# Up projections that alternate between two PSUM banks, warm-up matmuls at the start, and a new order in the last attention's output projection

## What is computed

```python
def swiglu(h, w_gu, w_down):
    gate, up = jnp.split(h @ w_gu, 2, axis=-1)
    return (jax.nn.silu(gate) * up) @ w_down

def mla_mixer(...):                     # the last attention
    ...
    s = (einsum(qn, k_nope) + einsum(qr, k_rope)) * scale
    s = where(key_pos <= q_pos, s, neg)
    p = softmax(s)
    o = einsum(p, v)                    # 8 heads of 128
    return o @ w_out                    # 1024 x 1024
```

## Time and profile before

| | us |
|---|---|
| median of three runs | 1383.79 (1381.64 to 1387.53) |
| the profiled execution | 1386.1 |
| its span, first to last instruction | 1384.3 |
| PE busy | 1358.3 (98%) |
| PEld busy | 1164.9 (84%) |
| DVE busy | 1120.5 (81%) |
| ACT busy | 786.3 (57%) |
| DMA, mean | 244 GB/s, 67% of 16 engines |

### The profile page before, as it was taken

The page is one execution under the profiler, slowest core; times in us unless marked ns, Lnnn a source line. Parts: engine busy times, 40 slices in busy tenths (PEclk is TensorE's granted clock), DMA queues, the critical chain, the costliest instruction groups (busy, mean ns, idle before and its releaser), DMA issues.

```text
span 1384.3 us, 19191 instructions
## 1 busy us (share of the span) xinstructions
PE 1358.3 (98%) x7512; PEld 1164.9 (84%) x7512; DVE 1120.5 (81%) x1652; ACT 786.3 (57%) x1155; POOL 1.4 (0%) x6
## 2 busy tenths in 40 slices
PE   6999999999999999999999999999999999999998
PEld 4988987888878888889888888888888997788886
DVE  8788687998988898879778888889888787796652
ACT  7713657676456555474485555476553746755542
POOL 0000000000000000000000000000000000000000
PEclk9999999999999999999999999999999999999999
DMA  9667435875948878777449878768789561575551
GB/s 378 268 213 278 146 124 186 280 254 196 342 190 305 294 282 310 298 247 271 169 168 329 295 286 333 273 250 316 275 292 366 192 228 62 198 259 183 191 195 40
DMA packets 63001, 337.77 MB, mean 244 GB/s; under 512 B 6960, under 2 KB 9392, under 8 KB 34752
## 3 DMA queue, kind: packets, MB, share of 16 engines
q1 hardware_dynamic: 62448, 335.35, 66.8%
q0 software_dynamic: 288, 1.05, 0.2%
q10 hardware_dynamic: 176, 0.16, 0.0%
HBM read 335.49 MB, written 1.05 MB: 243 GB/s over the span
## 4 chain that ended last, share of the span: by engine, by line
PE 90%; DVE 4%; ACT 3%; DMA 2%; issue 1%; SPq 0%; ACTq 0%; DVEq 0%
PE bank L317 88%; DMA raw<-w_stream 2%; DVE wlo L313 1%; ACT rstd L700 1%; ACT T L798 1%; PE bank L655 1%; DVE X L892 1%; PE bank L950 1%; PE bank L1080 0%; ACT whi L295 0%; DVE SGC L873 0%; PE bank L2409 0%; DVE XN L833 0%; ACT whi L269 0%; DVE mring L975 0%
## 5 line engine op out<-in xcount | busy, mean ns | idle before, releaser
L317 PE MATMUL bank<-hh,whi 128*128 128x512 f32 (+1 forms) x2160 | 665.1, 369 | 2.6 <-DVE hh L575 1.9
L317 PE MATMUL bank<-hh,wlo 128*128 128x256 f32 x1896 | 528.5, 280 | 0.0
L313 DVE TENSOR_TENSOR wlo<-raw,whi 128x2048 fp32r<-128x2048 f32 x197 | 449.9, 2286 | 39.9 <-ACT whi L295 39.6
L317 PEld LDWEIGHTS bank<-hh,whi 128*128 128x128 f32 x2160 | 387.9, 190 | 79.8 <-DVE wlo L313 3.4
L295 ACT ACTIVATE whi<-raw 128x2048 fp32r<-128x2048 f32 x197 | 376.4, 1915 | 120.6 <-PE bank L317 66.6
L317 PEld LDWEIGHTS bank<-hh,wlo 128*128 128x128 f32 x1896 | 357.6, 189 | 0.0
L317 PE MATMUL bank<-whi,hid_hi 128*128 128x512 f32 x440 | 172.2, 391 | 0.0
L317 PE MATMUL bank<-whi,hid_lo 128*128 128x512 f32 x440 | 171.3, 389 | 0.0
L317 PE MATMUL bank<-wlo,hid_hi 128*128 128x512 f32 x440 | 171.2, 389 | 0.0
L975 DVE SCALAR_TENSOR_TENSOR mring<-mring,con 128x1024 f32<-128x1024 f32 x107 | 130.2, 1219 | 12.5 <-DMA mring<-m_stream 12.5
L1162 ACT ACTIVATE GU<-bank 128x512 f32<-128x512 f32 x100 | 59.2, 592 | 113.2 <-PE bank L317 113.2
(11 more groups left out here) (332 smaller groups left out, 1436.0 us busy)
## 6 DMA issues: line engine op xcount, KB each, us to landing
raw<-w_stream SPq DMA_DIRECT2D x217, 1024.0 KB, 5.2
mring<-m_stream SPq DMA_DIRECT2D x139, 512.0 KB, 5.0
cb<-m_stream SPq DMA_DIRECT2D x53, 512.0 KB, 5.2
raw<-w_stream SPq DMA_DIRECT2D x4, 512.0 KB, 7.4
con<-const_d SPq DMA_DIRECT2D x1, 1472.0 KB, 15.2
XF<-xT SPq DMA_DIRECT2D x1, 1024.0 KB, 13.1
XC<-ctxT SPq DMA_DIRECT2D x1, 1024.0 KB, 10.2
y<-OUT SPq DMA_DIRECT2D x4, 256.0 KB, 2.6
```

The costliest lines, as they stand in the source:

```text
L313: nc.vector.tensor_tensor(w_lo(c, 0, CW), raw[:, c % RAW_SLOTS], w_hi(c, 0, CW).bitcast(f32), ALU.subtract).then_inc(s_lo, 1)
L317: return nc.tensor.matmul(out, lhsT, rhs, start=start, stop=True, skip_group_check=True)
```

## The change

1. In `pe_ffn`, k is now the outer loop. Per k, PE issues the rounded weights of gate and of value (512 columns each, two banks), then both weight rests (256 columns each). The wait for the copy of bank 5 stands ahead of the whole of t = 2.
2. Matmuls whose result nobody reads: five over 256 columns of zeros (`ut`, 36 rows) before the first real matmul, and four of `ident` with x after `turn_x(3)`.
3. In the last attention, DVE makes the rest of head 5 before it waits for the last head's exponentials; the rest of chunk c+1 comes between the rests of heads 6 and 7; the three conditioning columns follow chunks c+3, c+4 and c+5 and not c+1, c+2 and c+3. PE finishes both g of one half of `out_first` for t = 0 before it waits for the other half's bank.

```diff
@@ pe_ffn
-                for m in range(2):
-                    if t == 2 and m:
-                        pe.wait_ge(s_ub, 2 * f + 2)
-                    for k in range(DT):
-                        ins = mm2(bank[up_pair(t) + m][:], c0 + t, m * DT + k, hh[:, k], k == 0)
+                if t == 2:
+                    pe.wait_ge(s_ub, 2 * f + 2)
+                for k in range(DT):
+                    for m in range(2):
+                        mm(bank[up_pair(t) + m][:], w_hi(c0 + t, (m * DT + k) * P, (m * DT + k + 1) * P),
+                           hh[:, k].rearrange("p a n -> p (a n)"), k == 0)
+                    for m in range(2):
+                        ins = mm(bank[up_pair(t) + m][:, 0:SEQ], w_lo(c0 + t, (m * DT + k) * P, (m * DT + k + 1) * P),
+                                 hhi[:, k], False)
@@ pe_lstm
+        def pe_fill(pe, b, w, src, times):
+            for _ in range(times):
+                mm(bank[b][:, 0:src.shape[-1]], w, src, True)
...
+            pe.wait_ge(s_zero, 1)
+            pe_fill(pe, 6, ut[:, 0:P], ut[:, 0:SEQ], 5)
             pe.wait_ge(s_c4, 1)
...
             turn_x(3)
             pe.wait_ge(s_xc, 3)
+            pe_fill(pe, 3, ident, XF[:, 0], 4)
             pe_first_chunks(pe, U["x1"], c)
@@ pe_mla
-            for g in range(2):
-                ins = out_first(g, 0)
+            for half in range(2):
+                pe.wait_ge(s_h, U["mla_y"] + 7 + half)
+                for g in range(2):
+                    ins = out_first(g, 0, half)
@@ dve_mla
+                if h == MLA_HEADS - 1:
+                    rest_head(h - 2)
...
-            for h in range(MLA_HEADS - 3, MLA_HEADS):
-                rest_head(h)
-            for j in range(1, 6):
+            rest_head(MLA_HEADS - 2)
+            dve_split(dve, c + 1)
+            rest_head(MLA_HEADS - 1)
+            for j in range(2, 6):
                 dve_split(dve, c + j)
-                mods(dve, int(j < 4))
+                mods(dve, int(j > 2))
```

More of the change, by code:

```diff
@@ L1305, in build @@
         X_BANKS = (4, 5, 6, 0)
+        s_zero = sem("zeros_set")
+        def pe_fill(pe, b, w, src, times):
+            for _ in range(times):
+                mm(bank[b][:, 0:src.shape[-1]], w, src, True)
         def pe_lstm(pe):
@@ L1630, in dve_lstm @@
             nc.vector.memset(gi[:], 0.0)
-            nc.vector.memset(ut[:], 0.0)
+            nc.vector.memset(ut[:], 0.0).then_inc(s_zero, 1)
             nc.vector.memset(mt[:], 0.0)
@@ L2420, in values, with out_first @@
                 mm(o[:, P:], v(1), PT[:, h % 2, 2 * P:], False).then_inc(s_pv, 1)
[L2422 to L2427, removed]
+            def out_first(g, t, half):
+                return mm3w(out_bank(t, half), c, g * D + half * 512, tok(hhi, g, t), tok(hlo, g, t), g == 0)
             scores(0)
@@ L2439, in pe_mla @@
                     pe.wait_ge(s_h, U["mla_y"] + 6)
-                    out_first(0, 1)
+                    for half in range(2):
+                        out_first(0, 1, half)
                 transposes(h)
@@ L2443, in pe_mla @@
                     values(h - 1)
-            out_first(1, 1)
+            for half in range(2):
+                out_first(1, 1, half)
             values(MLA_HEADS - 1)
-            for g in range(2):
-                ins = out_first(g, 0)
+            for half in range(2):
+                pe.wait_ge(s_h, U["mla_y"] + 7 + half)
+                for g in range(2):
+                    ins = out_first(g, 0, half)
             ins.then_inc(s_pe, 1)
```

## The result

| | before | after |
|---|---|---|
| median, us | 1383.79 (1380.59 to 1387.53, 11 runs) | 1389.7 (1386.73 to 1391.63, 11 runs) |
| ratio to before | | 1.004, interval 1.0027 to 1.0052 |
| the profiled execution, us | 1386.1 | 1390.19 |
| its span, us | 1384.3 | 1388.1 |
| PE busy | 1358.3 (98%) | 1361.5 (98%) |

The change costs 5.5 us (0.0040 x 1383.8), with an interval of 3.7 to 7.2. The forecast was 1382.0, a little faster. The measured time lies inside the range of 1372 to 1391 but on the other side of no change; its ratio's interval straddles the 0.5% that the forecast took as the least that can be told from no change.

A forecast was written before the change was run, and what follows sets the result against it. PE was taken as the bound, with 90% of the chain of waits. Terms -6.3 + 2.7 + 2.3 - 1.0 - 0.6 = -2.9 us gave 1380.9 in the median's terms; the forecast said 1382, range 1372 to 1391.

The forecast's parts named there:

- Order of the matmuls: Up projections: fewer changes of matmul size let every section run at 347 ns a pair, -6.3 us.
- The wait ahead of t = 2: Up projections f0, f1, f2, f4: PE now waits uncovered for bank 5's copy, 0.67 us each, +2.7 us.
- The wait in f3: Up projection f3: late copy starts PE later, partly recovered in mid-chunk and at t = 7, +2.3 us.
- D: Rival: the clock falls to half behind f3's new stand, up to 1.7 us, giving 1384; chance 0.05.
- Fillers: Start of kernel: extra matmuls keep the full clock in the half-clock window near 35 us, -1.0 us.
- Last attention: Last attention's end: ACT rounds earlier, so DVE's closing chain of rests and columns ends earlier, -0.6 us.
- A: Rival: all five up projections keep the slow 353 ns rhythm, +7.5 us in sum, 1391.3; chance 0.18.
- C: Rival: alternating banks in the up projections speeds up matmuls, 21 us more gain, about 1360; chance 0.13.
- E: Rival: cycling banks in the up projections costs clock, +53 us, 1435; chance 0.02.
- B: Rival: up projections run half-way between the rhythms, 350 ns a pair, +2.4 us in sum, 1386.2; chance 0.20.

The follow-up runs named there:

- wait_only: Kernel before with only the wait for bank 5's copy moved ahead of all of t = 2, old matmul order; 1395.88 us, ratio 1.0073.
- fillers: Kernel before with only the two groups of matmuls whose result nobody reads; 1385.55 us, ratio 0.9993.
- mla_only: Kernel before with only the new order of the last attention; 1386.16 us, ratio 0.9995.
- order_t3: Kernel before with the new matmul order for t = 3 to 21 only, t = 2 and its waits as before; 1383.09 us, ratio 0.9983.
- twos_same_bank: Kernel before with matmuls in twos of one size for t = 3 to 21, both of a two in one bank; 1383.33 us, ratio 0.998.
- pairs_two_banks: Kernel before with 512 and 256 columns still alternating for t = 3 to 21, but the bank changing every pair; 1383.81 us, ratio 0.999.
- after_f3_old: Changed kernel with only f3's t = 2 back in the old order with its two waits; 1385.52 us, ratio 0.9999 to before.
- after_t2_old: Changed kernel with t = 2 of every up projection back in the old order with its two waits; 1383.27 us, ratio 0.9979 to before.
- order_all: Kernel before with only item 1 of the change, the up projections' new order and early wait; 1389.68 us, ratio 1.0041.
- after_again: The changed kernel run once more, unaltered; 1389.88 us, ratio 1.0038 to before.
- after_pairs: Changed kernel with t = 2 as before and, from t = 3, pairs of 512 and 256 columns to the two banks in turn; 1385.55 us, ratio 1.0009 to before.
- after_f3_fill: Changed kernel with f3's first t = 2 matmul issued 13 times more during the wait for bank 5's copy; 1387.4 us, ratio 1.0015 to before.

## Why the prediction was wrong

**Order of the matmuls, -6.3.** The step that failed is the value of the new rhythm: I took 347 ns a pair as the sum of both one-size runs, and said that halving the downward steps "lets PE keep the fast rhythm or at worst leaves the slow one". It does neither; it makes a rhythm of 348.3 ns. Over five sections that is 5 x 0.51 = 2.5 us less gain: -3.8 against the profiled execution. The reference was a second risk, which here cost little. The profiled execution of before is one draw, and the four profiled kernels that keep the old order from t = 3 on (before, wait_only, fillers, mla_only) hold 20 such sections, of which 11 took 107.4 us or more and 9 took 105.4 or, with a wait, 106.05. f1 was slow in all four; the others differ from profile to profile (f4 is slow in mla_only, f2 in wait_only). With that share the new order's mean gain is 11/20 x 1.52 less 9/20 x 0.51 = 0.6 us a section, 3.0 in all; against the profiled execution alone it is 3.2, and order_t3 measured 2.4, with an interval of 0.7 to 3.9. No kernel with the old order was profiled twice, so that its rhythm changes from execution to execution is inferred. Two things speak for it. Five profiled kernels have the same code up to t = 2 of f0, and four took 5.64 us there (before, order_t3, twos_same_bank, mla_only), but pairs_two_banks 5.54. And the times of before spread more on one chip (standard deviation 2.1 us) than those of order_t3 (1.3) and twos_same_bank (0.9). The forecast did see that "runs differ from each other by which sections fall into the slow rhythm", but used it only to choose between 1381 and 1383. The eight profiled kernels with sizes in twos have 40 sections of 105.85 to 105.88 us (first matmul's start to the last one's), or 106.48 where f3 waits at t = 7: the new order is steady, and that is its whole merit.

**The wait ahead of t = 2, +2.7 for four.** Right in mechanism and 0.1 us too small for each: 0.77 in f1's rows, since PE starts 0.14 us after the copy's end and not 0.05. Net of the 0.11 that t = 2 gains, four are 2.6 us by the rows and 2.8 by the ratios of after_f3_old and after_t2_old.

**The wait in f3, +2.3.** The mechanism and the stand were right: start at 913.67, later by 3.32 us against 3.24 forecast, and the wait at t = 7 is gone. The step that failed is the price of nothing that the sum put on the clock behind the stand, and D's chance of 0.05. I had the earlier trace rows, where a stand of 1.91 us was followed by a window at 0.50, and treated a stand of 3.4 us as unlikely to do the same. It did so in all four profiles that have it unfilled (the changed kernel twice, order_all, wait_only), and in none without. D's price of 1.7 us was also no upper bound: the half clock lasted 6.82 us in after_again. So this wait cost 3.32 + 0.99 + 0.11 - 0.58 = 3.8 us in the profiled pair (start, longer t = 2, its gain from the order, wait at t = 7 gone), where the sum had 2.3. The Trainium skill's page "TensorE: Matmul & The Clock Gate", in the table of its section "Why this matters for your kernels", warns against gaps between bursts of matmuls in which PE is idle. The trace agrees: a stand of 3.36 us, then a granted clock of 0.50. The forecast named that table and still gave it no weight.

**Fillers, -1.0.** The mechanism holds in every profile: the seven with fillers keep full clock near 35 us, the seven without lose it. The size is half of it by the profiled pair, 0.50 us, since PE then stands for DVE's chunk rest; averaged over the profiles, the seven with fillers reach the end of f0's token-wise chunks 0.8 us earlier than the seven without, two of which (order_all, pairs_two_banks) were at half clock for 6.82 us there. The ratio's -1.0 (interval -2.9 to +1.0) can't tell these apart.

**Last attention, -0.6.** Right: -0.7 up to the norm's transposes in each of the seven profiles that have the new order, for the reason given, that DVE's chain sets the end; the ratio's -0.7 can't be told from nothing. What the forecast left out is that PE now stands 2.2 us there, in all seven, and the clock may fall behind it: it did in two of the seven (mla_only and after_pairs), and in these PE came to f4 0.8 and 0.5 us later than with the old order, not 0.7 earlier.

**The term that was missing.** A PE that ends f0's up projection earlier does not always reach f1 earlier. In the changed profile 1.19 us went at the end of f0's down projection, where the last chunk came from memory late. In after_f3_fill and after_f3_old, the same code up to there, nothing was lost, and in after_again the norm's transposes began 2.11 us after the last matmul, and 1.9 us went. So this is a loss that comes in some executions; what makes the transfer late wasn't tried. A second stand of this kind, ahead of the norm behind f3's down projection, took 0.67 us more than before.

Rivals: A (slow rhythm in all sections) did not occur. C fell with twos_same_bank: the bank gives no speed. E did not occur either, and with it what the Trainium skill's page "TensorE: Matmul & The Clock Gate" tells in its section "A second HAM failure mode: psum-queue depth-cycling": order_t3 alternates banks at every one of 3040 matmuls, and the granted clock is 1.00 in its row above for f1 and in its four other sections too. What happened is the forecast's case with a rhythm part of the way to B's 350 ns, and D on top. The sum's -2.9 misses the +3.8 of the profiled pair's spans by 6.7 us: 2.5 for the rhythm, 1.5 for f3's wait with its clock, 1.9 for the two stands that no term held, 0.5 for the start and 0.4 for the four other waits. The first two alone would have brought the sum to +1.1, so they lost the sign.

## What to carry to other kernels

Before a gain is booked against one profile, ask whether what it shows is the same in every execution: a rhythm that two of five equal stretches have and three have not may fall otherwise in the next one. When a wait is moved ahead of work that covered it, the price is its length and then the clock behind it: a PE stand of several microseconds should be filled with throw-away matmuls, or better not made; here t = 2 in its old order with everything else changed (1383.27, ratio 0.9979) was faster than both kernels. Taking one part out of a change that bundles several is what showed this.

## What the runs showed of the hardware

- Alternating matmuls of 512 and 256 columns run at 347 or at 353 ns a pair, with the same work beside them and at full clock; a wait of about 0.43 us at f3's t = 7 moved PE from the first to the second for the rest of the section in before, mla_only and after_pairs, and a like one (0.41 us in fillers, 0.42 in pairs_two_banks) did not. In twos of one size they take 348.3 ns, in 40 of 40 sections. What sets the rhythm is open.
- The granted clock was 0.50, for 3.41 or 6.82 us, behind all four profiled PE stands of 3.4 us that were left empty. Of fifteen places where PE starts a norm's transposes 2.1 to 2.9 us after its last matmul, it fell at four; and it fell once, at 401.56 us of the changed profile, behind shorter stands (0.99, 0.52 and 0.44 us). What decides it there is open.
- Matmuls whose result is overwritten keep the clock as well: with thirteen of them it stayed at 1.00 through the same wait.
- ACT began the last raw chunk of f0 between 385.52 and 390.68 us over fourteen profiles, although PE ends the up projection before it within about 3 us (335.11 to 338.30). In four of them with the same code up to there (the changed kernel twice, after_f3_fill, after_f3_old) it was 387.08 to 389.84, with the up projection's end within 0.12 us.
